# Queries of the attention heads formed transposed, copied out by ScalarE and rotated on VectorE behind the keys

## The chip, the core and the metric

The kernel runs on one core of one Trainium2 chip. Its engines run side by side and wait for each other by semaphores: TensorE (PE in the profile; PEld is its weight load), VectorE (DVE), ScalarE (ACT), GpSimd (POOL) and SyncE (SP), which issues most DMAs. The metric is the device time of one execution in microseconds (us), lower is better.

## The reference, cut to what matters

One inference step of a hybrid encoder layer: 512 prompt tokens and 32 sample tokens, model width 1024, 8 heads with two query and two key parts of 64 each (q1|q2, k1|k2) and values of 128, float32.

```
z = rms_norm(x) @ w_in            # pool branch 512 | q 1024 | k 1024 | v 1024 | gate logits 2048
q = rope_partial(q)               # first 16 of every 64 dims: x1*cos - x2*sin, x2*cos + x1*sin
k = rope_partial(k)               # k and v are outputs too (new_k, new_v); q is not
a = softmax(q1 k1) - lam * softmax(q2 k2)      # 64-token chunks, block-causal mask
attn = a @ v                      # then per-head RMSNorm
merged = sigmoid(g_A) * (pool_y @ w_pool_branch) + sigmoid(g_B) * (attn @ w_attn_branch)
x = x + merged @ w_out
x = x + hier_moe(rms_norm(x))     # 16 experts, 2 per token
```

## The kernel before, in words

Every float32 product is made of three: each operand is split into a high part (rounded to the `fp32r` type, by ScalarE) and a low part (the rest, by VectorE), and `three` (L1748 to L1750) adds high·high, high·low and low·high in PSUM. PSUM has eight banks of 512 float32 columns by 128 partitions (`ps`).

The order of work is written out by hand, one program for each engine, tied by counting semaphores. The stages are: the norm and the transposed activations `hTh`/`hTl` (channels on partitions, 544 tokens along the row); pool branch and first gates; the eight heads; the second gates; output projection; routing; the experts.

**Projection of a head** (`project(h, j)`, j = 0 to 7, 128 input channels each). For each of five token tiles (four of the prompt, tile 4 with the 32 sample tokens, through `dec`) the tokens are the stationary operand and the head's 384 columns q|k|v of the weights the moving one: 3 matmuls of 384 columns for tiles 0 to 3, 2 for tile 4, so 14 for each j and 112 for a head. Tile t accumulates in bank t; ScalarE copies each bank out (`evacuate`, L804) to `qkv`, tokens on partitions. VectorE adds the low half of the sample rows (`join_sample`, L1313) and rotates queries and keys together (`rope`, L1324 to L1329: six operations of 128x160).

**Attention of the head before it.** While PE projects head h, attention of head h-1 goes on in banks 5 to 7, between the tiles: `turn` transposes queries and keys (11 transposes, L1915 to L1922), ScalarE and VectorE split them (`attend`), `scores` (L1935) forms the logits of three groups of tiles, VectorE takes maxima, ScalarE exponentials (`exponentials`, L837), VectorE subtracts the second map (`probs`, L1284), `turn_probs` (L1944) transposes the probabilities, ScalarE and VectorE split them (`probs_hi` L826, `probs_lo` L1307), and `values` (L1953, L1954) multiplies by the values. The end of head h-1 reaches into the projection of head h+1: `values` of its second group stand behind tile 0 of j=0, `turn_probs` of the third group behind tile 4 of j=0, and `values` of the third behind tile 3 of j=1:

```
project(h, 0, {0: lambda: values(h - 2, 1), NT - 1: lambda: turn_probs(h - 2, 2)})
project(h, 1, {3: lambda: values(h - 2, 2)})
turn(h - 1)
```

Engines execute in program order, so on VectorE `probs_lo(h-2, 2)`, which `values(h-2, 2)` waits for, stands between `join_sample(h-1)` and `rope(h-1)`. PE may write tile t of head h only when its bank's copy is done (`acc_ev`), and tile 4 when `join_sample` is done as well (`dec_done`). Heads 2 to 6 run in a hardware loop; heads 0, 1 and 7 are written out. After the last projection come the blocks of the second gates (`gate_block`), of which the first writes banks 0 and 1.

## Time and profile before

| | us |
|---|---|
| median of 3 runs | 845.56 (845.19 to 846.67) |
| span of the profiled execution | 843.6 |
| one head in the loop, on PE | 28.52 (230.91 to 259.43 of the span) |
| PE busy | 821.1 (97%) |
| DVE busy | 588.7 (70%) |
| ACT busy | 512.7 (61%) |

The profile is of one execution. The times of the runs are some 2 us longer than its span, since they hold what lies around the first and last instruction. Matmuls are pipelined: the busy time of one (0.34 us for 384 columns) is about twice its distance to the next, and what a matmul costs a full PE is that distance.

### The profile page before, as it was taken

To read this page: it belongs to the slowest core of one execution; us is meant where nothing else is said; L and a number is where in the kernel's file an instruction comes from. 1 tells how busy PE (TensorE), PEld (TensorE's weight loads), DVE (VectorE), ACT (ScalarE), POOL (GpSimd) and SP (SyncE) were. 2 spreads that over 40 slices of the span, in tenths; PEclk is the share of its full clock that TensorE was granted. 3 is DMA by queue.
4 is the path that set the end of the run, shared out by engine and by line. 5 is a ranking of instruction groups with operands and counts; after the bars stand their busy time and mean duration, and the time that the engine had idled before them with its cause. 6 is when DMAs were issued, how large, how long until landed. Compare 5 with 4: busy or idle time off the path is not lost.

```text
span 843.6 us, 15839 instructions
## 1 busy us (share of the span) xinstructions
PE 821.1 (97%) x5378; PEld 748.1 (89%) x5378; DVE 588.7 (70%) x957; ACT 512.7 (61%) x935; POOL 87.6 (10%) x76
## 2 busy tenths in 40 slices
PE   8999999999999999999999999999999999999992
PEld 7999999999999999999999888888888888888881
DVE  6373332777677768467467126999989999989995
ACT  7343313666566656565525233488888887888884
POOL 0000000000000000000000001222223322223112
PEclk9999999999999999999999999999999999999996
DMA  9632213232133213332234746699999999999925
GB/s 274 139 103 83 67 44 95 82 109 75 36 104 107 59 54 108 102 101 75 79 123 157 270 177 204 236 371 372 380 377 374 368 368 367 364 368 367 351 70 193
DMA packets 135959, 163.54 MB, mean 194 GB/s; under 512 B 18599, under 2 KB 103719, under 8 KB 135914
## 3 DMA queue, kind: packets, MB, share of 16 engines
q1 hardware_dynamic: 129674, 149.53, 52.7%
q0 software_dynamic: 5952, 12.82, 5.4%
q8 instruction: 28, 0.46, 0.2%
q10 hardware_dynamic: 288, 0.59, 0.2%
q14 instruction: 17, 0.14, 0.1%
HBM read 151.61 MB, written 20.12 MB: 204 GB/s over the span
## 4 chain that ended last, share of the span: by engine, by line
PE 52%; DVE 3%; DMA 2%; issue 1%; ACT 1%; POOLq 0%; POOL 0%; ACTq 0%
PE ps L1748 15%; PE ps L1750 15%; PE ps L1749 15%; PE ps L2182 2%; PE ps L2094 1%; DMA xg<-sum_rows,idi 1%; PE ps L2101 1%; PE ps L2204 1%; DMA sum_rows<-yb,ydn 1%; PE ps L2086 0%; PE ps L2127 0%; PE ps L2128 0%; PE ps L2025 0%; DVE wl L1144 0%; PE ps L1953 0%
## 5 line engine op out<-in xcount | busy, mean ns | idle before, releaser
L1623 DVE TENSOR_TENSOR wl<-rawM,wh 128x1024 fp32r<-128x1024 f32 x189 | 223.9, 1220 | 14.3 <-ACT wh L980 12.4
L980 ACT ACTIVATE wh<-rawM 128x1024 fp32r<-128x1024 f32 x192 | 195.8, 1057 | 6.2 <-PE ps L1750 2.8
L1748 PE MATMUL ps<-hTh,wh 128*128 128x272 f32 (+2 forms) x448 | 131.0, 292 | 1.4 <-ACT qkv L804 1.0
L1750 PE MATMUL ps<-hTh,wl 128*128 128x272 f32 (+2 forms) x448 | 129.5, 289 | 0.0
L1749 PE MATMUL ps<-hTl,wh 128*128 128x272 f32 (+2 forms) x448 | 128.9, 288 | 0.0
L1748 PE MATMUL ps<-wh,xh 128*128 128x256 f32 (+1 forms) x384 | 124.3, 324 | 0.3 <-DVE xl L1669 0.3
L1750 PE MATMUL ps<-wh,xl 128*128 128x256 f32 (+1 forms) x384 | 121.7, 317 | 0.0
L1749 PE MATMUL ps<-wl,xh 128*128 128x256 f32 (+1 forms) x384 | 121.6, 317 | 0.0
L1748 PE MATMUL ps<-wh,hTh 128*128 128x384 f32 x256 | 90.0, 352 | 0.2 <-DVE mA L1254 0.2
L1748 PEld LDWEIGHTS ps<-hTh,wh 128*128 128x128 f32 x448 | 84.3, 188 | 3.0 <-ACT qkv L804 1.3
L1750 PE MATMUL ps<-wh,hTl 128*128 128x384 f32 x256 | 86.3, 337 | 0.0
L1749 PE MATMUL ps<-wl,hTh 128*128 128x384 f32 x256 | 86.0, 336 | 0.0
L1749 PEld LDWEIGHTS ps<-hTl,wh 128*128 128x128 f32 x448 | 84.4, 188 | 0.0
L1750 PEld LDWEIGHTS ps<-hTh,wl 128*128 128x128 f32 x448 | 84.3, 188 | 0.0
L1748 PEld LDWEIGHTS ps<-wh,xh 128*128 128x128 f32 x384 | 72.1, 188 | 9.9 <-issue 3.9
L1144 DVE TENSOR_TENSOR wl<-rawA,wh 128x1024 fp32r<-128x1024 f32 (+2 forms) x41 | 47.7, 1169 | 43.5 <-ACT wh L691 43.3
L1750 PEld LDWEIGHTS ps<-wh,xl 128*128 128x128 f32 x384 | 72.4, 188 | 5.8
L1749 PEld LDWEIGHTS ps<-wl,xh 128*128 128x128 f32 x384 | 72.3, 188 | 5.8
L691 ACT ACTIVATE wh<-rawA 128x1024 fp32r<-128x1024 f32 (+2 forms) x41 | 41.1, 1018 | 45.4 <-PE ps L1750 30.1
L605 POOL DMA_INDIRECT sum_rows<-yb,ydn x15 | 37.7, 2514 | 192.4 <-issue 167.0
L614 POOL DMA_DIRECT2D h_rows<-hb x4 | 2.4, 602 | 519.5 <-DVE hb L1484 519.5
L1748 PE MATMUL ps<-wh,hh 128*128 128x512 f32 x128 | 53.2, 415 | 0.6 <-DVE hl L1638 0.6
(324 smaller groups left out, 1711.5 us busy)
## 6 DMA issues: line engine op xcount, KB each, us to landing
rawM<-in_w_expert_up SPq DMA_DIRECT2D x64, 512.0 KB, 9.2
rawM<-in_w_expert_down SPq DMA_DIRECT2D x64, 512.0 KB, 8.0
rawM<-in_w_expert_gate SPq DMA_DIRECT2D x64, 512.0 KB
rawA<-in_w_in SPq DMA_DIRECT2D x64, 192.0 KB, 3.0
rawA<-in_w_in SPq DMA_DIRECT2D x20, 512.0 KB, 5.3
rawA<-in_w_attn_branch SPq DMA_DIRECT2D x8, 512.0 KB, 3.5
rawA<-in_w_out SPq DMA_DIRECT2D x8, 512.0 KB, 4.2
x<-in_x_prompt SPq DMA_DIRECT2D x4, 512.0 KB, 6.7
```

The source lines that it names most:

```text
L605: pool.indirect_dma_start(acc_rows[:, :], bass.IndirectOffsetOnAxis(ap=ydn[:, par:par + 1], axis=0), yb[:, par, :], None, bounds_check=TOK ...
L691: nc.scalar.activation(split_slot(n)[0][:, 0:w], rawA[:, n % RA, 0:w], ACT.Copy).then_inc(hi_done, 1)
L980: nc.scalar.activation(wh[:, (c + 1) % S, :], rawM[:, slot, :], ACT.Copy).then_inc(m_hi, 1)
L1144: V.tensor_tensor(l[:, 0:w], rawA[:, n % RA, 0:w], h[:, 0:w].bitcast(F32), ALU.subtract).then_inc(lo_done, 1)
L1623: V.tensor_tensor(wl[:, sl, :], rawM[:, slot, :], wh[:, sl, :].bitcast(F32), ALU.subtract).then_inc(m_lo, 1)
L1748: T.matmul(out, sh, mh_, start=start, stop=False, **kw)
L1749: T.matmul(out, sh, ml_, start=False, stop=False, **kw)
L1750: return T.matmul(out, sl, mh_, start=False, stop=stop, **kw)
L2094: ins = T.matmul(ps[:, 6 + m, 20 * i:20 * i + 20], h2T[:, 4 * (s % 2) + k, :], wr[:, 4 * m + k, :], start=k == 0, stop=k == 3)
L2101: T.matmul(ps[:, bank, :], one, many, start=True, stop=True)
L2182: ins = T.transpose(ps[:, 2 + k // 4, P * (k % 4):P * (k % 4 + 1)], xg[:, par, P * k:P * k + P], id_m)
L2204: ins = T.transpose(ps[:, 4, P * k:P * k + P], hid[:, P * k:P * k + P], id_m)
```

## The change: what it does

The queries leave the token-tile product. `queries(j, half)` takes the head's 128 query columns of the weights as stationary operand and 272 tokens of `hTh`/`hTl` as moving one, so queries come out transposed (dims on partitions, 544 tokens along the row) in banks 3 and 4. `keys_values(j, t)` does k|v, 256 columns, two token tiles to a bank (banks 0, 1, 2). `copy_queries` (ScalarE) copies both query banks to `q_turned`. The rotation of the queries is `swap_queries` and `turn_queries` on VectorE: two products of 128x544 with tables of cosines and signed sines, a `stream_shuffle` that swaps the two halves of 8 rows within each 32 partitions, and a sum. The tables (`q_cos`, `q_sin`, 544 columns each) are loaded once, ahead of the first cached keys. `rope` now rotates the keys alone (128x80), the transposes of the queries are gone from `turn`, and the splits of the values stand behind those of queries and keys. On VectorE `rope` and `swap_queries` now stand ahead of `probs_lo(h-2, 2)`. The copy of bank 0 waits for tiles 0 and 1. The hooks of `project` keep their numbers. Semaphores of the row loads are shared with the last stage's, which changes no order.

```diff
-        qkv = hr("qkv", [P, NT, 384])
+        kv = hr("kv", [P, NT, KV])
...
+        q_turned, q_swap, q_cos, q_sin = (at(n, 170 * K + 4 * TOK * b, [P, TOK]) for n, b in (
+            ("q_turned", 4), ("q_swap", 5), ("q_cos", 6), ("q_sin", 7)))
...
+        def kv_bank(t):
+
+            return ps[:, t // 2, KV * (t % 2):KV * (t % 2 + 1)]
...
+            sp.dma_start(q_cos[:], a["cst"][:, C_QCOS:C_QCOS + TOK]).then_inc(qt_in, 16)
+            sp.dma_start(q_sin[:], a["cst"][:, C_QSIN:C_QSIN + TOK]).then_inc(qt_in, 16)
...
-            def evacuate(h, tiles=range(NT)):
-
-                for t in tiles:
-                    if t < 4:
-                        act.wait_ge(acc_mm, 4 * h + t + 1)
+            def copy_queries(h):
+
+                act.wait_ge(q_mm, h + 1)
+                if not (isinstance(h, int) and h == 0):
+                    act.wait_ge(tr_lo, 2 * h)
+                nc.scalar.activation(q_turned[:].rearrange("p (h n) -> p h n", h=2), ps[:, 3:5, 0:HALF],
+                                     ACT.Copy).then_inc(q_ev, 1)
+
+            def evacuate(h, banks=range(NEV)):
+
+                for b in banks:
+                    if b < 2:
+                        act.wait_ge(acc_mm, 2 * h + b + 1)
                     else:
                         act.wait_ge(mm_done, H0 + 4 * h + 4)
-                    if t == 0 and not (isinstance(h, int) and h == 0):
+                    if b == 0 and not (isinstance(h, int) and h == 0):
                         act.wait_ge(kv_out, 64 * h)
                         act.wait_ge(tr_lo, 2 * h)
                         act.wait_ge(vlo_done, h)
-                    nc.scalar.activation(qkv[:, t, :], ps[:, t, 0:384], ACT.Copy).then_inc(acc_ev, 1)
+                    n = len(KV_TILES[b])
+                    nc.scalar.activation(kv[:, 2 * b:2 * b + n, :], ps[:, b, 0:KV * n].rearrange("p (t c) -> p t c", t=n),
+                                         ACT.Copy).then_inc(acc_ev, 1)
...
-                act.wait_ge(acc_ev, NT * (g + 1))
+                act.wait_ge(q_done, g + 1)
+                nc.scalar.activation(qh[:], q_turned[:], ACT.Copy).then_inc(q_hi, 1)
+                act.wait_ge(acc_ev, NEV * (g + 1))
                 if not (isinstance(g, int) and g == 0):
                     act.wait_ge(av_mm, NGR * g)
                 act.wait_ge(ckv_in, 32 * (g + 1))
                 act.wait_ge(dec_done, g + 1)
-                nc.scalar.activation(vh[:, 0:NT, :], qkv[:, :, 2 * P:3 * P], ACT.Copy)
-                nc.scalar.activation(vh[:, NT, :], ckv[:, 1, :], ACT.Copy).then_inc(vhi_done, 1)
                 act.wait_ge(tr_mm, 2 * g + 1)
-                nc.scalar.activation(qh[:, 0:SEQ], ps[:, 5, :], ACT.Copy)
                 nc.scalar.activation(kh[:], ps[:, 6, :], ACT.Copy).then_inc(tr_hi, 1)
                 act.wait_ge(tr_mm, 2 * g + 2)
-                nc.scalar.activation(qh[:, SEQ:TOK], ps[:, 7, LAST:P], ACT.Copy)
-                nc.scalar.activation(kth[:], ps[:, 7, P:3 * P], ACT.Copy).then_inc(tr_hi, 1)
+                nc.scalar.activation(kth[:], ps[:, 7, 0:2 * P], ACT.Copy).then_inc(tr_hi, 1)
+                nc.scalar.activation(vh[:, 0:NT, :], kv[:, :, P:KV], ACT.Copy)
+                nc.scalar.activation(vh[:, NT, :], ckv[:, 1, :], ACT.Copy).then_inc(vhi_done, 1)
...
+            def first_copies(h):
+
+                copy_queries(h)
+                evacuate(h, (0,))
...
             def join_sample(g):
 
-                dve.wait_ge(acc_ev, NT * (g + 1))
-                V.tensor_tensor(qkv[LAST:P, 4, :], ps[2 * DEC:LAST, 4, 0:384], qkv[LAST:P, 4, :],
+                dve.wait_ge(acc_ev, NEV * (g + 1))
+                V.tensor_tensor(kv[LAST:P, 4, :], ps[2 * DEC:LAST, 2, 0:KV], kv[LAST:P, 4, :],
...
+            def swap_queries(g, lk):
+
+                if isinstance(g, int) and g == 0:
+                    dve.wait_ge(qt_in, 32)
+                dve.wait_ge(q_ev, g + 1)
+                lk(V.tensor_tensor(q_swap[:], q_turned[:], q_sin[:], ALU.mult))
+                V.tensor_tensor(q_turned[:], q_turned[:], q_cos[:], ALU.mult)
+                lk(V.stream_shuffle(q_swap[:], q_swap[:], HALF_SWAP))
+
+            def turn_queries(g):
+
+                V.tensor_tensor(q_turned[:], q_turned[:], q_swap[:], ALU.add).then_inc(q_done, 1)
...
                 join_sample(h - 1)
+                rope(h - 1, lk)
+                swap_queries(h - 1, lk)
                 if not first:
                     probs_lo(h - 2, 2)
-                rope(h - 1, lk)
+                turn_queries(h - 1)
                 lo_head(2, n + 2)
...
+            def queries(j, half, sl, q0):
+
+                tc = slice(HALF * half, HALF * (half + 1))
+                return three(ps[:, 3 + half, 0:HALF], wh[:, sl, q0:q0 + P], wl[:, sl, q0:q0 + P], hTh[:, j, tc], hTl[:, j, tc],
+                             j == 0, j == KD - 1)
+
+            def keys_values(j, t, sl, q0):
+
+                wc, first = slice(q0 + P, q0 + 3 * P), j == 0 and t % 2 == 0
+                if t < 4:
+                    return three(kv_bank(t), hTh[:, j, col(t)], hTl[:, j, col(t)], wh[:, sl, wc], wl[:, sl, wc],
+                                 first, j == KD - 1, skip_group_check=True)
+                both = dec[:, 2 * DEC * j:2 * DEC * j + P]
+                T.matmul(kv_bank(t), both, wh[:, sl, wc], start=first, stop=False)
+                return T.matmul(kv_bank(t), both, wl[:, sl, wc], start=False, stop=j == KD - 1)
...
             def project(h, j, after={}):
 
                 n = H0 + 4 * h + j // 2
-                sl, k = (H0 + j // 2) % S, j % 2
-                if k == 0:
+                sl, q0 = (H0 + j // 2) % S, 384 * (j % 2)
+                if j % 2 == 0:
                     pe.wait_ge(lo_done, n + 1)
-                wc = slice(384 * k, 384 * k + 384)
+                if j == KD - 1:
+                    queries(j, 0, sl, q0)
+                    queries(j, 1, sl, q0).then_inc(q_mm, 1)
                 for t in range(NT):
-                    if j == 0:
-                        pe.wait_ge(acc_ev, NT * (h - 1) + t + 1)
+                    if j == 0 and t % 2 == 0:
+                        pe.wait_ge(acc_ev, NEV * (h - 1) + t // 2 + 1)
                         if t == 4:
                             pe.wait_ge(dec_done, h)
-                    if t < 4:
-                        ins = three(ps[:, t, 0:384], hTh[:, j, col(t)], hTl[:, j, col(t)], wh[:, sl, wc], wl[:, sl, wc],
-                                    j == 0, j == KD - 1)
-                    else:
-                        both = dec[:, 2 * DEC * j:2 * DEC * j + P]
-                        T.matmul(ps[:, t, 0:384], both, wh[:, sl, wc], start=j == 0, stop=False)
-                        ins = T.matmul(ps[:, t, 0:384], both, wl[:, sl, wc], start=False, stop=j == KD - 1)
-                    if j == KD - 1 and t < 4:
+                    ins = keys_values(j, t, sl, q0)
+                    if j == KD - 1 and t in (1, 3):
                         ins.then_inc(acc_mm, 1)
-                    if t == NT - 1 and k == 1:
+                    if j == KD - 1 and t == NT - 1:
                         ins.then_inc(mm_done, 1)
                     if t in after:
                         after[t]()
+                if j < KD - 1:
+                    if j == 0:
+                        pe.wait_ge(q_ev, h)
+                    queries(j, 0, sl, q0)
+                    ins = queries(j, 1, sl, q0)
+                    if j % 2:
+                        ins.then_inc(mm_done, 1)
 
...
-                for m in range(2):
-                    for t in range(4):
-                        ins = T.transpose(ps[:, 5 + m, P * t:P * t + P], qkv[:, t, P * m:P * m + P], id_m)
+                for t in range(4):
+                    ins = T.transpose(ps[:, 6, P * t:P * t + P], kv[:, t, 0:P], id_m)
                 ins.then_inc(tr_mm, 1)
                 if not (isinstance(g, int) and g == 0):
                     pe.wait_ge(av_ev, NGR * g)
-                for m in range(2):
-                    T.transpose(ps[:, 7, P * m:P * m + P], qkv[:, 4, P * m:P * m + P], id_m)
+                T.transpose(ps[:, 7, 0:P], kv[:, 4, 0:P], id_m)
                 pe.wait_ge(ckv_in, 32 * (g + 1))
-                T.transpose(ps[:, 7, 2 * P:3 * P], ckv[:, 0, :], id_m).then_inc(tr_mm, 1)
+                T.transpose(ps[:, 7, P:2 * P], ckv[:, 0, :], id_m).then_inc(tr_mm, 1)
...
-                if b < 2:
-                    pe.wait_ge(acc_ev, NT * (HEADS - 1) + 2 * b + 2)
+                if b == 0:
+                    pe.wait_ge(acc_ev, NEV * (HEADS - 1) + 2)
+                elif b == 1:
+                    pe.wait_ge(acc_ev, NEV * HEADS)
+                    pe.wait_ge(dec_done, HEADS)
+                    pe.wait_ge(q_ev, HEADS)
```

**VectorE, start of a head's body in the loop** (`project` of head h on PE; kv and rot are of head h-1, atl is the low part of the third group's probabilities of head h-2). Before:

```order
L1313 TENSOR_TENSOR qkv<-ps,qkv 32x384 [waits acc_ev]
L1307 TENSOR_TENSOR atl<-ps,ath 128x512 [waits ath_done]
L1324 TENSOR_TENSOR rot<-qkv,cst 128x160 [waits dec_done]
L1325 TENSOR_TENSOR rot<-qkv,cst 128x160
L1326 TENSOR_TENSOR rot<-qkv,cst 128x160
L1327 TENSOR_TENSOR rot<-qkv,cst 128x160
...
L1328 TENSOR_TENSOR qkv<-rot 128x5x4x8 [waits dve_chain]
L1329 TENSOR_TENSOR qkv<-rot 128x5x4x8
...
L1260 TENSOR_TENSOR wl<-rawA,wh 128x768 [waits hi_done]
```

and now:

```order
L1351 TENSOR_TENSOR kv<-ps,kv 32x256 [waits acc_ev]
L1375 TENSOR_TENSOR rot<-kv,cst 128x80 [waits dec_done]
L1376 TENSOR_TENSOR rot<-kv,cst 128x80
L1377 TENSOR_TENSOR rot<-kv,cst 128x80
L1378 TENSOR_TENSOR rot<-kv,cst 128x80
...
L1379 TENSOR_TENSOR kv<-rot 128x5x2x8 [waits dve_chain]
L1380 TENSOR_TENSOR kv<-rot 128x5x2x8
L1359 TENSOR_TENSOR q_swap<-q_turned,q_sin 128x544 [waits q_copied]
...
L1360 TENSOR_TENSOR q_turned<-q_turned,q_cos 128x544 [waits dve_chain]
L1361 STREAM_SHUFFLE q_swap<-q_swap 128x544
...
L1345 TENSOR_TENSOR atl<-ps,ath 128x512 [waits ath_done,dve_chain]
L1365 TENSOR_TENSOR q_turned<-q_turned,q_swap 128x544
```

The low part of the probabilities stood second, behind the sum of the sample rows; now six operations of the keys' rotation and three of the queries' stand ahead of it.

**ScalarE, end of the same body** (ps to qkv, kv and q_turned are copies out of the projection of head h; ath and E are of head h-1). Before:

```order
L801 REGISTER_ALU [waits acc_mm]
L802 REGISTER_ALU [waits kv_out]
L804 ACTIVATE qkv<-ps 128x384 [waits vlo_done,tr_lo]
...
L826 ACTIVATE ath<-ps 128x512 [waits ta_mm]
...
L837 ACTIVATE E_86,esum<-ps,nb 128x512 [waits nb_done]
...
L837 ACTIVATE E_86,esum<-ps,nb 128x512 [waits nb_done]
...
L804 ACTIVATE qkv<-ps 128x384 [waits acc_mm]
...
L804 ACTIVATE qkv<-ps 128x384 [waits acc_mm]
...
L804 ACTIVATE qkv<-ps 128x384 [waits acc_mm]
```

and now:

```order
L819 REGISTER_ALU [waits q_mm]
L820 ACTIVATE q_turned<-ps 128x544 [waits tr_lo]
...
L831 REGISTER_ALU [waits acc_mm]
L835 ACTIVATE kv<-ps 128x512 [waits vlo_done,tr_lo,kv_out]
...
L858 ACTIVATE ath<-ps 128x512 [waits ta_mm]
...
L869 ACTIVATE E_86,esum<-ps,nb 128x512 [waits nb_done]
...
L869 ACTIVATE E_86,esum<-ps,nb 128x512 [waits nb_done]
...
L835 ACTIVATE kv<-ps 128x512 [waits acc_mm]
...
L835 ACTIVATE kv<-ps 128x256 [waits mm_done]
```

Ahead of the split of the probabilities stood one copy of 384 columns, which waited for tile 0; now two copies of 544 and 512 columns stand there, and the second waits for tile 1. Behind the exponentials two copies are left of four.

**PE, the transposes between the second and third product of a head** (cst is the identity). Before:

```order
L1915 MATMUL ps<-cst,qkv 128x128 [waits exp_done]
L1915 MATMUL ps<-cst,qkv 128x128 x7
L1920 MATMUL ps<-cst,qkv 128x128 [waits av_ev]
L1920 MATMUL ps<-cst,qkv 128x128
...
L1922 MATMUL ps<-cst,ckv 128x128 [waits ckv_in]
```

and now:

```order
L1805 MATMUL ps<-hTh,wl 128x272
L1983 MATMUL ps<-cst,kv 128x128 [waits exp_done,rope_done]
L1983 MATMUL ps<-cst,kv 128x128 x3
L1987 MATMUL ps<-cst,kv 128x128 [waits av_ev]
...
L1989 MATMUL ps<-cst,ckv 128x128 [waits ckv_in]
```

Ten transposes of queries and keys have become five of keys alone; the cached keys' one stays, and a query matmul stands directly ahead.

## Rows read from the trace of the kernel before

**Rows 1.** The page's first part: busy time, share of the span, instructions of each engine.
```profile
PE 821.1 (97%) x5378; PEld 748.1 (89%) x5378; DVE 588.7 (70%) x957; ACT 512.7 (61%) x935; POOL 87.6 (10%) x76
```

**Rows 2.** The waits of PE over the span, third row: total, times, longest (us).
```profile
PE ps L1748 <- ACT qkv L804: 1.0, 1, 1.0
```

**Rows 3.** Windows: one period of the head loop; stretch, sum, busy by engine, clock, DMA.
```profile
230.91:259.43 28.52, 28.52 (x190) 26.59 (x189) 21.55 (x57) 18.31 (x59) 0.00 (x0) 1.00 0.28 79
```

**Rows 4.** Timeline, PE: start, us, engine, line; ten adjoining matmuls of 384 columns.
```profile
256.41 0.33 PE L1750 MATMUL ps<-wh,hTl 128*128 128x384 f32 x1
...
257.99 0.34 PE L1750 MATMUL ps<-wh,hTl 128*128 128x384 f32 x1
```

**Rows 5.** Timeline, PE: thirteen adjoining matmuls of 256 columns, weights as moving operand.
```profile
544.34 0.28 PE L1749 MATMUL ps<-wl,xh 128*128 128x256 f32 x1
...
545.70 0.28 PE L1749 MATMUL ps<-wl,xh 128*128 128x256 f32 x1
```

**Rows 6.** Timeline, PE: fourteen adjoining matmuls of 272 columns, gate logits.
```profile
340.27 0.29 PE L1749 MATMUL ps<-hTl,wh 128*128 128x272 f32 x1
...
341.90 0.29 PE L1750 MATMUL ps<-hTh,wl 128*128 128x272 f32 x1
```

**Rows 7.** Timeline, PE: twenty-four adjoining matmuls of 256 columns, activations as moving operand.
```profile
21.07 0.28 PE L1748 MATMUL ps<-hTh,wh 128*128 128x256 f32 x1
...
23.79 0.28 PE L1750 MATMUL ps<-hTh,wl 128*128 128x256 f32 x1
```

**Rows 8.** Timeline, PE: the transposes of one head's queries and keys.
```profile
259.43 1.04 PE L1915 MATMUL ps<-cst,qkv 128*128 128x128 f32 x8
260.31 0.38 PE L1920 MATMUL ps<-cst,qkv 128*128 128x128 f32 x2
```

**Rows 9.** Timeline, PE: from one head's last tiles to the next head's second product.
```profile
249.60 0.34 PE L1750 MATMUL ps<-wh,hTl 128*128 128x384 f32 x1
...
250.31 0.60 PE L1944 MATMUL ps<-cst,E 128*128 128x128 f32 x4
250.66 0.42 PE L1748 MATMUL ps<-wh,hTh 128*128 128x384 f32 x1
...
252.69 0.28 PE L1953 MATMUL ps<-vv,ath 128*128 128x256 f32 x1
...
253.57 0.39 PE L1748 MATMUL ps<-wh,hTh 128*128 128x384 f32 x1
...
258.16 0.28 PE L1953 MATMUL ps<-vv,ath 128*128 128x256 f32 x1
```

**Rows 10.** Timeline, ACT: the same stretch.
```profile
250.19 0.49 ACT L804 ACTIVATE qkv<-ps 128x384 f32<-128x384 f32 x1 [2.48 <-PE ps L1750]
250.94 0.60 ACT L826 ACTIVATE ath<-ps 128x512 fp32r<-128x512 f32 x1 [0.26 <-PE ps L1944]
251.44 0.68 ACT L837 ACTIVATE E<-ps,nb 128x512 f32<-128x512 f32 x1
...
252.76 1.64 ACT L804 ACTIVATE qkv<-ps 128x384 f32<-128x384 f32 x4
```

**Rows 11.** Timeline, DVE: the same stretch.
```profile
253.37 0.75 DVE L1284 SCALAR_TENSOR_TENSOR E<-E,ratio 128x512 f32<-128x512 f32 x1
254.44 0.56 DVE L1313 TENSOR_TENSOR qkv<-ps,qkv 32x384 f32<-32x384 f32 x1 [0.32 <-ACT qkv L804]
256.88 0.69 DVE L1307 TENSOR_TENSOR atl<-ps,ath 128x512 fp32r<-128x512 f32 x1 [1.88 <-ACT ath L826]
257.49 0.32 DVE L1324 TENSOR_TENSOR rot<-qkv,cst 128x160 f32<-128x160 f32 x1
...
259.02 0.95 DVE L1260 TENSOR_TENSOR wl<-rawA,wh 128x768 fp32r<-128x768 f32 x1
```

**Rows 12.** Groups of DVE instructions by line and form: count, busy us, mean ns.
```profile
L1334 DVE TENSOR_TENSOR vv<-qkv,vv 128x640 fp32r<-128x640 f32 x8 | 6.5, 819 | 3.4 <-ACT vv L850 3.4
...
L1335 DVE TENSOR_TENSOR vv<-ckv,vv 128x128 fp32r<-128x128 f32 x8 | 2.3, 287 | 0.0
```

109 lines of the change are left out of this document (60 added, 49 removed).

## The prediction

> **What bounds the kernel now.** I read the page's busy times first: PE is busy 97% of the span, VectorE 70%, ScalarE 61% [rows 1]. Then PE's waits: in the whole heads stage the only one listed is 1.0 us, once, where the first gate block needs the copies of banks 0 and 1 [rows 2]. A period of the head loop is 28.52 us with PE busy throughout, VectorE 21.55 and ScalarE 18.31, the clock granted in full [rows 3]. So today the stage is the sum of PE's own work, and the others have 7 and 10 us of air. But a mean says nothing about when. The timelines of the three engines side by side do: around the seam between two heads they form one long chain, from the last tiles of a head through the exponentials to `values` of the third group [rows 9 to 11]. That chain ends just in time today, and the change both lengthens it and shortens the PE work that covers it.
>
> **PE's own work, matmuls.** What one costs is the distance between starts. 384 columns: 1.58 us over 9 steps, 0.176 us [rows 4]. 256 columns with weights as the moving operand, which is the form of keys and values: 1.36 over 12 steps, 0.113 [rows 5]. 272 columns of activations, which is the form of the queries: 1.63 over 13, 0.125 [rows 6]. A 256-column form elsewhere takes 2.72 over 23, 0.118 [rows 7]. One input slice before is 14 x 0.176 = 2.46 us. After, it is 14 of 256 and 6 of 272: with 0.113, 1.59 + 0.75 = 2.34; with 0.118, 2.41. I take 0.115, since rows 5 have the operands of the new form: 2.36, a saving of 0.10 us. There are 8 slices in each of 8 heads: 6.2 us gained (3.2 to 7.7).
>
> A rule speaks against this step. The Trainium skill ("TensorE: Matmul & The Clock Gate", Back-to-back issue gap) gives a sustained 81 ns at 128 columns and 131 ns at 512 where each matmul loads weights, so much of the cost would not depend on width. My estimate from its straight line: 98 ns at 256, 100 at 272, 114 at 384, so a slice would go from 1.60 to 1.97 us and the 64 slices cost 24 us. The trace disagrees: 0.113 and 0.176 us stand nearly as 256 to 384 [rows 4, 5].
>
> **PE's own work, transposes.** `turn` loses five of its eleven. Eight took 0.88 us from start to the next kind, 0.11 each [rows 8]. 8 x 5 x 0.11 = 4.4 us gained. Matmuls and transposes together: 10.6 us, if PE never waits.
>
> **The chain at the seam.** Let T be the start of `turn_probs` of the second group, 250.31 [rows 9].
>
> ScalarE before: the copy of tile 0 starts 0.59 after the last matmul it waits for (249.60 to 250.19), is done early, and the split of the probabilities starts at T+0.63 [rows 9, 10]. After: the copy of bank 0 waits for tile 1, the last work ahead of T. A 256-column matmul is 0.06 shorter (0.28 against 0.34 [rows 5, 9]), so it starts 0.53 after a matmul that began at T-0.11: T+0.42. The copy of the queries stands ahead of it, but its product is 0.7 us older and it is over by then. A 512-column copy holds ScalarE 0.50 (250.94 to 251.44 [rows 10]). So the split starts at T+0.92 and the exponentials at T+1.42.
>
> VectorE: the map's subtraction ends 2.68 after the exponentials start (253.37 + 0.75 - 251.44 [rows 10, 11]): T+4.10. The next operation may start 0.08 before an unrelated one ends (256.88 + 0.69 against 257.49 [rows 11]). One more column costs 1.04 ns, (819 - 287)/512 [rows 12]. `join_sample`, 128 columns shorter than 0.56: T+4.02 to 4.45. The keys' rotation, six operations, took 1.53 (257.49 to 259.02 [rows 11]), and each loses 80 columns: 1.03, from T+4.48 to 5.51. A 544-column product is 0.287 + 416 x 1.04 ns = 0.72 [rows 12]. The first is waited for (0.04 more, from such pairs as the one above): T+6.27. The second, overlapping its follower by 0.08: T+6.91. The shuffle is not in the trace. Its nearest rows are those same sizes: 0.72 and the wait 0.04, T+7.67. Bounds: 0.29, the row of 128 columns, below [rows 12]; twice 0.72 above. Then the low split, 0.69 [rows 11]: T+8.36, and `values` can start at T+8.39.
>
> The Trainium skill ("VectorE: DVE Perf Modes", The perf-mode tier table) gives a shuffle of 2048 elements about 2400 ns where it gives the two-tensor product 2293, whatever the permutation. By that the shuffle is 0.1 us dearer than I take it, an estimate, and the time 0.6 us longer over six heads. No row here shows a shuffle.
>
> PE before: from T to `values` of the third group is 7.85 us (250.31 to 258.16 [rows 9]): 34 matmuls of 384 at 0.176 = 5.97, two `turn_probs` of 0.35, one `values` of 0.88 (252.69 to 253.57 [rows 9]), and 0.30 left over at changes of kind. The low split ended at 257.57, 0.6 ahead [rows 11]. PE after: 34 x 0.115 = 3.91, six query matmuls 0.75, and 0.70 + 0.88 + 0.30 as before: 6.54. So PE is there at T+6.54 and must wait until T+8.39: **1.85 us for each head.** Parts of it show earlier, and are in that sum, not beside it: `values` of the second group is wanted at about T+1.7, but its low split ends at 0.92 + 0.60 + 0.03 + 0.69 = T+2.24 [rows 10, 11], some 0.5 us; tile 4 is wanted near T+4.2 and the sample rows are joined at 4.45, some 0.3; the rest, about 1.0, at `values` of the third group.
>
> This hook runs in heads 2 to 7, six times: 11.1 us lost. Net for such a head: 0.8 + 0.55 gained, 1.85 lost, a period of 29.0 against 28.52.
>
> **Behind heads.** The first gate block waits for the second copy. Before that was over at T+2.94 (252.76 + 0.49, taken from the same seam), PE came at about T+1.9, hence the 1.0 us [rows 2, 10]. After, exponentials at T+1.42, the copy 1.32 later, 0.60 long: T+3.34, and PE comes at about T+1.4, since it has 0.5 us less to do: 1.0 us lost more.
>
> **Costed at nothing.** Behind the third `values`, VectorE has the queries' sum, a weight split, the two clamps and the low parts of queries and keys ahead of the first scores, some 4.0 us at these sizes; PE has `values`, tile 4, a query part, six transposes and a slice, 4.9. The value splits that moved back feed only the second half of the body. If that cover went it would cost the difference per head, up to 0.5. VectorE's total grows by some 2 us to 23.6 of 29.0, ScalarE's falls (one 544 copy and three, 1824 columns, for five, 1920). The two tables stand ahead of the first cached keys in SP's queue, under a DMA share of 0.28 [rows 3]: nothing, or some tenths once. Head 1 has no `values` and its seam should only close up.
>
> **Sum.** 843.6 - 6.2 - 4.4 + 11.1 + 1.0 = 845.1 for the profiled execution, 1.5 above its 843.6. The median lies 2.0 above that span, so 847.1.
>
> **Rivals.**
> - *Shorter chain.* If the rotation's operations on SBUF alone, small copies or waits are cheaper than read off and the chain from T to `values` is 7.6 instead of 8.4, each head waits 0.8 less: 842.3. For: I extrapolate four operations of 544 columns and six of 80. Against: the row of 640 columns is itself all in SBUF [rows 12]. The point from which the kernel is faster at all is a chain of T+8.1, so this is near. If VectorE were ready at T+6.54 nothing is lost in the loop, and 10.6 is gained: 835.0. That needs 1.85 us off the chain; the shuffle for nothing gives 0.76.
> - *The shuffle costs double.* 0.76 more for each of six heads, all of it on the chain: 851.7.
> - *A fixed part in each matmul.* If the new forms go at 0.118 [rows 7] the gain of the slices is 3.2 and not 6.2, but PE comes 0.1 later to each wait, 0.7 back: 849.4. Twenty matmuls for fourteen is what speaks for it. (The skill's rule above is the extreme of this; the trace leaves it no chance worth a number.)
> - *Waits pull the clock down.* Three waits of up to 1 us in each period; yet the present 1.0 us wait is followed at once by 272-column matmuls at 0.125 us, the full level [rows 2, 6]. No chance of its own.
>
> **Chances.** My forecast as worked out 0.55, from 844.3 to 850 for itself (0.3 of an us on the chain is 1.8 on the time); the shorter chain 0.17; no waits 0.05; double shuffle 0.11; fixed part 0.12. A measurement of this kernel tells about 0.2%, 1.7 us, from no change, so the line between same and slower is 847.25 and runs through my forecast. Slower: 0.27 of the forecast's share, 0.11 and 0.09: 0.47. Same: 0.22, 0.02, 0.03: 0.27. Faster: 0.06, 0.15, 0.05: 0.26. The range 842 to 851.5 leaves out the case without waits and the far halves of the short chain and of the double shuffle.
>
> **What would show it.** Starts of the 256-column matmuls 0.113 to 0.118 apart, of the query ones 0.125; five transposes of kv; PE waits named in the loop, where there were none: at `values` for atl, and at tile 4 for the joined rows, 1.85 us together; a loop period of 29.0; the shuffle near 0.72 us; the first gate block waiting about 2 us. The forecast is wrong if the loop period is at or below 28.5, if PE still shows no waits at the seam, or if the low split starts before T+7.4 because the operations ahead of it are shorter.

## The result, and the profile after

The changed kernel takes **851.1 us** (median of 4 runs, 850.92 to 851.65) against 846.1 of the kernel before on the same chip (845.19 to 846.77): ratio 1.0064, 95% interval 1.0052 to 1.0076, slower by 5.0 us. The forecast was 847.1, 1.5 slower. The side was right and the time lies in the range, 0.4 below its upper end, but the move is three times the one forecast. The profiled spans are 849.1 and 843.6, 5.5 apart.

The page's busy times after, for [rows 1]:

```profile
PE 817.7 (96%) x5722; PEld 746.3 (88%) x5722; DVE 606.2 (71%) x989; ACT 512.0 (60%) x919; POOL 87.5 (10%) x76
```

PE is busy 3.4 us less in a span 5.5 us longer. The waits of PE over the span (total, times, longest), for [rows 2]:

```profile
PE ps L2020 <- DVE atl L1345: 6.5, 12, 0.8
PE ps L1803 <- ACT kv L835: 1.6, 1, 1.6
```

A wait of the loop that was not there before heads the list: `values` (L2020) for the low split of the probabilities (`atl`), twice for each of six heads. The wait at the first gate block grew from 1.0 to 1.6. One period of the loop, `turn` to `turn`, for [rows 3] (stretch, length, busy by engine, clock, DMA):

```profile
233.55:263.09 29.54, 28.28 (x235) 26.48 (x234) 23.94 (x61) 18.33 (x57) 0.00 (x0) 1.00 0.27 77
```

A head takes 29.54 against 28.52, and 29.0 was forecast. The clock is granted in full in both. From `turn` to `turn` by the starts of PE's transposes, the first six periods sum to 176.98 us where they were 171.14: +5.84. The stretch ahead of the first `turn` is 0.23 shorter, the last period, with the first gate blocks, 0.21. So the loop holds the whole loss.

The seam between two heads on PE's timeline (idle time in brackets, and who ended it), for [rows 9]:

```profile
252.55 0.60 PE L2011 MATMUL ps<-cst,E 128*128 128x128 f32 x4
...
254.18 0.28 PE L1805 MATMUL ps<-wh,hTl 128*128 128x256 f32 x1
254.77 0.39 PE L2020 MATMUL ps<-vv,ath 128*128 128x256 f32 x1 [0.31 <-DVE atl L1345]
...
256.75 0.28 PE L1805 MATMUL ps<-wh,hTl 128*128 128x256 f32 x1
257.17 0.35 PE L1926 MATMUL ps<-wh,dec 128*128 128x256 f32 x1
...
259.99 0.28 PE L1805 MATMUL ps<-wh,hTl 128*128 128x256 f32 x1
261.07 0.38 PE L2020 MATMUL ps<-vv,ath 128*128 128x256 f32 x1 [0.80 <-DVE atl L1345]
```

Between starts, where 0.12 would pass without a wait, there are 0.59, 0.42 and 1.08 us: three delays of 0.47, 0.30 and 0.96 (the bracket names a part of the first and last, and none at tile 4), at the three places that the prediction named. And VectorE's in the same seam, for [rows 11]:

```profile
255.82 0.75 DVE L1322 SCALAR_TENSOR_TENSOR E<-E,ratio 128x512 f32<-128x512 f32 x1
256.60 0.42 DVE L1351 TENSOR_TENSOR kv<-ps,kv 32x256 f32<-32x256 f32 x1
257.06 0.24 DVE L1375 TENSOR_TENSOR rot<-kv,cst 128x80 f32<-128x80 f32 x1
...
258.10 0.72 DVE L1359 TENSOR_TENSOR q_swap<-q_turned,q_sin 128x544 f32<-128x544 f32 x1
258.86 0.73 DVE L1360 TENSOR_TENSOR q_turned<-q_turned,q_cos 128x544 f32<-128x544 f32 x1
259.51 0.01 DVE L1361 LOAD_MASK_SELECT q_swap<-q_swap  x1
259.51 0.78 DVE L1361 STREAM_SHUFFLE q_swap<-q_swap 128x544 f32<-128x544 f32 x1
260.32 0.69 DVE L1345 TENSOR_TENSOR atl<-ps,ath 128x512 fp32r<-128x512 f32 x1
```

There is no gap over 0.04 from the subtraction to the low split. With T = 252.55, the start of `turn_probs` of the second group as in the prediction, the split ends at T+8.46 and `values` starts at T+8.52; the forecast had T+8.36 and T+8.39. The chain was forecast to 0.13 us, so the size of the loss must come from the other side: from PE's own time.

### The profile page after: what moved, and what is told of

Its sections match the earlier page's. It is cut to its first block, busy times and chain, and to the rows that moved or that the text cites. A ratio compares the mean times of both kernels' runs of the same rounds, so it can differ in the third digit from the quotient of the medians.

```text
span 849.1 us, 16545 instructions
## 1 busy us (share of the span) xinstructions
PE 817.7 (96%) x5722; PEld 746.3 (88%) x5722; DVE 606.2 (71%) x989; ACT 512.0 (60%) x919; POOL 87.5 (10%) x76
## 4 chain that ended last, share of the span: by engine, by line
PE 52%; DVE 2%; DMA 2%; ACT 1%; issue 1%; POOLq 0%; POOL 0%; ACTq 0%
PE ps L1803 15%; PE ps L1805 15%; PE ps L1804 15%; PE ps L2252 2%; DMA xg<-sum_rows,idi 1%; PE ps L2164 1%; PE ps L2171 1%; PE ps L2274 1%; DMA sum_rows<-yb,ydn 1%; PE ps L2156 0%; PE ps L2197 0%; PE ps L2198 0%; PE ps L2095 0%; DVE wl L1182 0%; DMA out_y_prompt<-ob 0%
## 5 line engine op out<-in xcount | busy, mean ns | idle before, releaser
L1803 PE MATMUL ps<-hTh,wh 128*128 128x272 f32 (+2 forms) x576 | 168.2, 292 | 2.2 <-ACT kv L835 1.6
L1805 PE MATMUL ps<-hTh,wl 128*128 128x272 f32 (+2 forms) x576 | 166.4, 289 | 0.0
L1804 PE MATMUL ps<-hTl,wh 128*128 128x272 f32 (+2 forms) x576 | 165.9, 288 | 0.0
L1803 PEld LDWEIGHTS ps<-hTh,wh 128*128 128x128 f32 x576 | 108.5, 188 | 3.7 <-ACT kv L835 1.8
L1804 PEld LDWEIGHTS ps<-hTl,wh 128*128 128x128 f32 x576 | 108.6, 188 | 0.0
L1805 PEld LDWEIGHTS ps<-hTh,wl 128*128 128x128 f32 x576 | 108.4, 188 | 0.0
L1803 PE MATMUL ps<-wh,hTh 128*128 128x256 f32 x256 | 75.4, 294 | 0.1
L1805 PE MATMUL ps<-wh,hTl 128*128 128x256 f32 x256 | 72.1, 282 | 0.0
L1804 PE MATMUL ps<-wl,hTh 128*128 128x256 f32 x256 | 72.0, 281 | 0.0
```

Source lines behind the costliest of these rows:

```text
L1803: T.matmul(out, sh, mh_, start=start, stop=False, **kw)
L1804: T.matmul(out, sh, ml_, start=False, stop=False, **kw)
L1805: return T.matmul(out, sl, mh_, start=False, stop=stop, **kw)
```

## Experiments

All ratios are to the kernel before. Each was timed on one chip together with it, except the two kernels with a row of idle products, which ran once. Each changes the changed kernel, unless it says otherwise, and "theory A" and "B" are those of the expectation above each result.

### Is it the rotation that TensorE waits for?

First without it:

```diff
-                lk(V.tensor_tensor(q_swap[:], q_turned[:], q_sin[:], ALU.mult))
-                V.tensor_tensor(q_turned[:], q_turned[:], q_cos[:], ALU.mult)
-                lk(V.stream_shuffle(q_swap[:], q_swap[:], HALF_SWAP))
...
-                V.tensor_tensor(q_turned[:], q_turned[:], q_swap[:], ALU.add).then_inc(q_done, 1)
+                dve.sem_inc(q_done, 1)
```

> The changed kernel without the rotation of the queries: the two products, the shuffle and the sum on VectorE are left out (queries go into the scores unrotated), 3.0 us of VectorE work for each head ahead of the low split that the third value group waits for. Theory A (the rotation stands ahead of that split and TensorE waits for it 0.97 us in each turn of the loop, and starts again some 0.1 us late): the wait at the third value group goes, the waits at the second value group (0.3 to 0.5 us) and at tile 4 (0.4 us) stay, a head takes 28.45 us in place of 29.53, six of them 6.4 us less: 844.7 us. Theory B (the wait is set by the transposes and ScalarE's copies, not by the rotation): no change, 851. With either, what the head takes beyond its waits tells the pace of the products: 28.45 less 0.85 of waits is 27.6 with 256-column products at 0.119 us, and would be 27.2 at the 0.115 that the forecast took.

Measured: **844.65 us**, ratio 0.9983 (0.9973 to 0.9993). PE's waits, and a period:

```profile
PE ps L2017 <- DVE atl L1345: 1.7, 6, 0.3
...
PE ps L1800 <- ACT kv L835: 1.6, 1, 1.6
```

```profile
230.37:258.84 28.47, 28.00 (x235) 26.41 (x234) 21.27 (x55) 18.31 (x57) 0.00 (x0) 1.00 0.28 79
```

Twelve waits have become six, those of the second value group; the wait at the third is gone, and with it 1.06 us a head (28.47 for 29.53). Theory A stands to the tenth. But with the rotation left out and 0.8 us of wait left (0.5 at the second value group, 0.3 at tile 4), a head takes as long as before the change: 28.47 against 28.52. By the forecast's sizes it should have been 28.0: 28.52 less 0.77 for the slices and 0.55 for the transposes, and 0.8 of waits.

Then with more of it, the first product made twice:

```diff
                 lk(V.tensor_tensor(q_swap[:], q_turned[:], q_sin[:], ALU.mult))
+                lk(V.tensor_tensor(q_swap[:], q_turned[:], q_sin[:], ALU.mult))
```

> The changed kernel with the first of the rotation's products (queries by sines, 128x544, 0.72 us) made twice. Theory A (all of the rotation lies on the path to the third value group's low split): each of six heads gets 0.75 to 0.8 us longer, 4.5 to 4.8 us in all: 855.7 us, and TensorE's wait there grows from 0.97 to 1.75. Theory B (something beside VectorE sets that wait): below 852.

Measured: **859.16 us**, ratio 1.0151 (1.0136 to 1.0165): 8.1 over the changed kernel where 4.6 was expected. The direction is theory A's, the size is not. PE's waits, two of the periods, and then stretches of about one microsecond around another head's third value group, which starts at 266.62 (the clock is the third number from the end):

```profile
PE ps L2021 <- DVE atl L1345: 10.9, 12, 1.5
```

```profile
208.12:238.38 30.26, 28.27 (x235) 26.46 (x234) 24.60 (x62) 18.40 (x57) 0.00 (x0) 1.00 0.26 75
...
269.38:300.47 31.09, 29.12 (x234) 27.31 (x234) 23.92 (x61) 17.80 (x56) 0.00 (x0) 0.97 0.26 73
```

```profile
265.50:266.62 1.12, 0.00 (x0) 0.00 (x1) 1.08 (x3) 0.00 (x0) 0.00 (x0) 1.00 0.69 184
266.62:267.60 0.98, 0.98 (x9) 0.98 (x9) 0.98 (x2) 0.00 (x0) 0.00 (x0) 1.00 0.00 0
...
268.60:269.60 1.00, 1.00 (x7) 1.00 (x6) 0.96 (x2) 0.53 (x1) 0.00 (x0) 0.50 0.00 0
...
270.60:271.60 1.00, 1.00 (x9) 1.00 (x8) 0.50 (x1) 1.00 (x3) 0.00 (x0) 0.74 0.00 0
```

Two of the six periods are 0.73 longer than in the changed kernel, as worked out. The other four are 1.5 to 2.0 longer, and their mean clock is 0.97 or 0.98: behind two of the six waits of 1.5 us the granted clock falls from 1.00 to 0.50, the lower level of 1.2 GHz, for some 3.5 us (1.7 us lost), and each fall lies across a `turn`, so that it lengthens two periods. It was not this execution alone: the mean clocks of the five runs are 0.988 to 0.990, those of the changed kernel 0.992. The changed kernel's waits of 0.8 are followed by the full clock in every period, so this is no part of its loss. It is why a little more on that chain can cost double.

### The same work in other orders

One step moved: the low split ahead of the queries' rotation, behind the keys' (and likewise in the written-out last head).

```diff
                 rope(h - 1, lk)
-                swap_queries(h - 1, lk)
                 if not first:
                     probs_lo(h - 2, 2)
+                swap_queries(h - 1, lk)
                 turn_queries(h - 1)
```

> The changed kernel with one step moved: the third group's low split of the probabilities stands behind the rotation of the keys and ahead of the rotation of the queries. Theory A: the wait at the third value group goes (0.97 and 0.1 of restart), the queries' own splits come 0.7 us later and the first scores wait 0.3 us for them: a head takes 28.8 us in place of 29.53, in all 846.7 us (846 to 848). Theory B (the first scores wait for all that the value group no longer waits for, since the rotation is only shifted): the same as the changed kernel, 851. Were the products at the forecast's pace, this order would have come to 842.

Measured: **850.16 us**, ratio 1.0050 (1.0037 to 1.0064). A period, PE's waits, and VectorE's timeline behind the seam:

```profile
232.08:261.28 29.20, 28.13 (x235) 26.42 (x234) 23.64 (x61) 18.40 (x56) 0.00 (x0) 1.00 0.28 77
```

```profile
PE ps L2002 <- ACT E L869: 2.0, 6, 0.4
PE ps L2020 <- DVE atl L1345: 1.7, 6, 0.3
...
PE ps L2002 <- DVE kl L1387: 1.5, 6, 0.3
```

```profile
258.01 0.69 DVE L1345 TENSOR_TENSOR atl<-ps,ath 128x512 fp32r<-128x512 f32 x1 [0.57 <-ACT ath L858]
258.62 0.71 DVE L1359 TENSOR_TENSOR q_swap<-q_turned,q_sin 128x544 f32<-128x544 f32 x1
...
262.35 0.55 DVE L1309 TENSOR_TENSOR att<-att,clamped 128x384 f32 x1
...
268.85 0.16 DVE L1338 SCALAR_TENSOR_TENSOR nb<-mx,shift 128x2 f32<-128x2 f32 x1
...
270.15 0.18 DVE L1317 RECIPROCAL rinv<-esum 128x4 f32<-128x4 f32 x1 [0.35 <-ACT E L869]
```

The wait at the third value group went as expected, and 0.3 us at the first scores came as expected. What neither theory had is 0.4 us more at the second scores (L2002, which wait for the exponentials `E`): 2.4 us over six heads of the 3.5 by which 846.7 became 850.2; nearly 1.0 more came in the last period, 37.6 for 36.65. The reason is in the third fence: from 258.01 to 269.8 VectorE works without a gap over 0.04, so whatever is put in at the front arrives at the first maxima (`nb` at 268.85), and through the exponentials at the second scores. The loop has two chains, seam to values and seam to scores, and the rotation stands on both.

A second reordering moved the first clamp behind the splits, bank 0's copy behind the high split, and the first slice's queries and third transposes ahead of tile 4:

> The changed kernel with the same work in another order. VectorE: the third group's low split ahead of the queries' rotation, and the first clamp behind the splits of queries, keys and values. ScalarE: the copy of bank 0 behind the high split of the second group. TensorE: in the first slice of a head the queries' products and the third group's transposes stand ahead of tile 4. Theory A (what the change lost to its three waits of 1.8 us and two restarts of 0.1 us can all be had back, and what is left is TensorE's own work): a head takes 27.6 us (27.4 to 27.9), in all 839.5 us (838.5 to 841.5). With 256-column products at the forecast's 0.115 it would take 27.2 and come to 837. Theory B (the waits come back at another place, the first scores or the copies of the banks): 28.5 us or more, 845 us.

Measured: **853.8 us**, ratio 1.0089 (1.0073 to 1.0104). PE's waits from the first `turn` to the last:

```profile
PE ps L2001 <- ACT E L869: 7.0, 6, 1.2
PE ps L1800 <- ACT kv L835: 3.4, 7, 2.0
```

Theory B held: the value groups wait no longer (no `atl` in the list), and the time is lost at the second scores, 1.2 us a head, since the clamp still stood ahead of the maxima; a head takes 29.43. The 2.0 in the second row is the first gate block's. Behind it the granted clock was 0.50 for some 3.5 us in this profiled execution, which at 856.4 was the slowest of the four. Two versions that put the maxima first of all, and the clamp and a weight split behind them, were slower still (VectorE's lines that differ from the reordering before):

```diff
-                nxt(3)
                 largest(g, 0, lk)
                 if not (isinstance(g, int) and g == 0):
+                    clamp(g - 1, 0, lk)
                     clamp(g - 1, 1, lk)
+                nxt(3)
```

> The changed kernel with the third group's low split ahead of the queries' rotation, and with VectorE's line behind it shortened: the first maxima stand right behind the values' splits, and the clamp of three tiles and the next weights' low split behind them (2.0 us of work that no longer stands ahead of the maxima); ScalarE takes its first three squares behind the first exponentials. Theory A (in the version with the split moved alone, TensorE waited 0.3 us at the first scores and 0.4 at the second, because VectorE works from the third group's split to the first maxima, 12 us, without a gap; it is this line and no longer the third value group that sets the loop): both waits go, a head takes 28.4 us (28.3 to 28.6) with the waits at the second value group and tile 4 left, in all 844.7 us (844 to 846). Theory B (the line of VectorE is not what the scores wait for, ScalarE's exponentials and squares are): no gain over 850.2.

> The same as the version with the maxima first, and besides: ScalarE copies bank 0 behind the high split of the second group, and TensorE does the first slice's query products and the third group's transposes ahead of tile 4. Theory A (what is left then is TensorE's own work, 27.6 to 27.8 us a head): 840.2 us (839 to 842), below the kernel before. Were 256-column products at the 0.115 us of the forecast, it would be 837 to 838. Theory B (the copies of the banks or VectorE's line take over again): a head at 28.4 or more, 844.5 us or more.

Measured: **858.12** and **859.0 us**, ratios 1.0146 (1.0130 to 1.0162) and 1.0147 (1.0129 to 1.0164). PE's waits in the first of the two:

```profile
PE ps L2018 <- DVE atl L1345: 6.5, 12, 0.8
PE ps L1801 <- DVE wl L1182: 5.4, 2, 5.2
```

The scores wait no more, but the 2 us of work put behind the maxima now stands ahead of the first group's probabilities, and the first value group waits 0.8; and in the written-out tail the gate block's weight split is the work put behind, 5.2 us of wait at once. During that wait the granted clock fell to 0.50, and it stayed there until 372.8, 4.0 us after the wait's end: 2.0 us more. Both expectations missed because I looked only at who waits behind the front of the line, not behind its rear.

The third reordering was counted along the whole line. The clamp goes behind the first maxima, but the weight split stays ahead of them, where it fills the time until the scores are done; the next head's weight split goes behind the first low split; the second group's transposes go one tile earlier; the tail keeps its order. In the main:

```diff
                 largest(g, 0, lk)
                 if not (isinstance(g, int) and g == 0):
+                    if not last:
+                        clamp(g - 1, 0, lk)
                     clamp(g - 1, 1, lk)
...
                     probs_lo(g, i - 1)
+                    if not last and i == 1:
+                        nxt(4)
...
-                project(h, 7, {1: lambda: turn_probs(h - 1, 1)})
+                project(h, 7, {0: lambda: turn_probs(h - 1, 1)})
```

> The changed kernel's work in a third order. VectorE: the third group's low split ahead of the queries' rotation; the clamp of three tiles behind the first maxima (1.1 us less ahead of them), and the next head's first weight split behind the first group's low split (0.95 us less ahead of that). ScalarE: bank 0 copied behind the high split of the second group, the first three squares behind the first exponentials. TensorE: the second group's transposes one tile earlier (behind tile 0 of the last slice), the first slice's query products and the third group's transposes ahead of tile 4. The last head's own attention keeps its order. Theory A (counted along VectorE's line from the version of the first reordering: maxima end 17.4 us behind the second group's transposes, where TensorE wants the second scores at 17.4; first group's low split 22.0, wanted 22.5): no wait over 0.1 us is left in the loop, a head takes 27.7 us (27.5 to 28.0), in all 840.3 us (839 to 842.5), below the kernel before. Theory B (VectorE with 23.7 us of work in a head of 27.7 can't be kept off TensorE's path in any order): a head at 28.5 or more, 845 or more.

> The same as the shortened line, and for the last head ScalarE copies bank 1 with bank 0, ahead of the third group's exponentials, so that the first gate block, which TensorE waits 1.6 us for, finds its banks copied. Theory A: that wait goes to 0.2 us, the exponentials come 0.5 us later at a place with slack: 1.4 us below the version it is made from, 839. Theory B (the last head's attention is on the path that ends the stage, so that the 0.5 us come back): no difference.

Measured: **842.74 us**, ratio 0.9966 (0.9954 to 0.9979), and with bank 1 copied early for the last head **841.37 us**, ratio 0.9950 (0.9936 to 0.9963). Both are below the kernel before, by 0.3% and 0.5%, with intervals that leave out 1, and below the changed kernel. The early copy did what was expected of it: the wait of the gate block fell from 1.7 to 0.5 and the time by 1.4. The second one's waits of PE from the first `turn` to the last, whole list, and a period:

```profile
PE ps L1808 <- ACT kv L835: 0.5, 1, 0.5
PE ps L2009 <- ACT E L869: 0.2, 1, 0.2
```

```profile
229.02:257.07 28.05, 27.96 (x234) 26.46 (x233) 23.53 (x61) 18.33 (x56) 0.00 (x0) 1.00 0.28 81
```

So theory A is right in kind: VectorE with 23.5 of 28 us can be kept off PE's path. Its number was not: 28.05 us is some 0.35 more than expected, though PE has next to nothing left to wait for in the loop (all gaps are 0.2 or less). This is the cleanest reading of PE's own work in the new form, and it is only 0.47 below the old one.

### What a product costs

Does the price of 256 columns show in the time, and not only in the starts on the trace?

```diff
+                    if 2 <= j < KD - 1 and t < 4:
+                        keys_values(j, t, sl, q0)
                     ins = keys_values(j, t, sl, q0)
```

> The changed kernel with the 256-column products of the four prompt tiles made twice in slices 2 to 6 of heads 1 to 7 (the sums of keys and values are wrong by that): 12 x 5 x 7 = 420 products of 256 columns more on TensorE, and nothing on the other engines. Theory A (256 columns with weights moving cost 0.1187 us here, as the trace of the changed kernel shows): 49.9 us more, less up to 1 us where the waits of the gate block and of the loop find more slack: 900.5 us. With the forecast's 0.115: 48.3 more, 899.2; at the 0.1133 of the long runs in the last stage: 47.6 more, 898.5. The distance of two products in the trace, read in these runs of 24, is the sharper number: A says 0.119 or more.

Measured: **908.91 us**, ratio 1.0744 (1.0729 to 1.0758), 57.8 over the changed kernel. The expectation counted heads 1 to 7; head 0 runs the same function, so it is 480 products: 57.8/480 = 0.120 us each. The period of the loop gives the same without the rest:

```profile
262.42:299.15 36.73, 35.47 (x295) 33.67 (x294) 23.92 (x61) 18.40 (x57) 0.00 (x0) 1.00 0.22 62
```

36.73 - 29.53 = 7.20 for 60 products, 0.120. The forecast's 0.115 and the 0.113 of [rows 5] are out.

Why two prices for one shape? A row of idle products (their results are not used), one stationary operand, no waits:

> The changed kernel with a row of idle products put at its start, where no other engine has much to do, all of the same operands: 24 of 512 columns, 36 of 256, 8 transposes, 36 of 256, 24 of 272, 36 of 256, 24 of 384, 36 of 256, 12 of 288, 12 of 128, 36 of 256. The kernel gets some 40 us longer; only the distances of the products are read. Theory A (a 256-column product has two paces by what ran before it: 0.1133 us behind a run of 512 columns, 0.1178 to 0.119 behind transposes or 272 columns, and keeps it until another shape comes): 0.1133 in the first run of 36 and 0.118 in the others. Theory B (the pace hangs on how busy ScalarE, VectorE and the memory are): one pace in all five runs of 36. Theory C (it hangs on the stationary operand's layout, which is one and the same here): one pace as well.

Measured by stretches, from the first start of a run to the first of what follows (PE's count is one or two high, for products that reach in from the sides):

```profile
13.84:18.14 4.30, 4.30 (x37) 4.30 (x36) 0.00 (x0) 0.00 (x0) 0.00 (x0) 1.00 1.10 352
...
23.33:26.33 3.00, 3.00 (x26) 3.00 (x25) 0.00 (x0) 0.00 (x0) 0.00 (x0) 1.00 0.13 32
26.34:30.63 4.29, 4.29 (x38) 4.29 (x37) 0.00 (x0) 0.00 (x0) 0.00 (x0) 1.00 0.74 23
30.64:34.80 4.16, 4.16 (x26) 4.16 (x25) 0.00 (x0) 0.00 (x0) 0.00 (x0) 1.00 0.12 7
```

36 of 256 columns take 4.30 us, 0.1195, behind 512 and 272 columns alike (rows one and three), and the same behind 384. Behind transposes they take 4.38, but the 0.08 lie in the first step alone (0.20), and the last transpose has 0.03 to the next start where the others have 0.11. 24 of 272 take 3.00, 0.125; 24 of 384 take 4.16, 0.1735. Theory A is wrong. B and C foresaw the one pace, and neither explains the 0.113 of [rows 5], which stays open. The steps between widths are 128 columns in 0.054 us and 16 in 0.0055, so from 256 columns up a product costs its columns and, on top, a fixed 0.013 us: 256 columns at the 2.4 GHz level are 0.107, 384 are 0.160. Below 256 this does not hold: in the same row 12 products of 128 columns take 1.28 us, 0.107 each, where columns (0.053) and 0.013 would be 0.066.

Then whole slices, five old and five new, in the same way:

> The changed kernel with a row of idle products at its start, no waits among them and one bank, the stationary operand changed as in the heads: five old slices (14 products of 384 columns each), five new ones (14 of 256 and 6 of 272), then five times 4 transposes with 14 products of 256 behind them, and five times 4 transposes with 14 of 384. Only distances are read. Theory A (each product costs its columns and a fixed part of 0.013 us, as the idle row before showed: 0.1737 us for 384 columns, 0.1196 for 256, 0.1254 for 272): an old slice takes 2.43 us and a new one 2.43 as well, so that the products gain nothing where the forecast had 0.097 a slice; behind transposes both widths lose the same 0.1 us. Theory B (the fixed part belongs to products of one width alone, or to the heads' own conditions): a new slice at 2.36, 0.07 or more below an old one.

```profile
7.46:19.61 12.15, 12.15 (x71) 1.00 1.08 315
19.63:31.74 12.11, 12.11 (x101) 1.00 0.38 20
...
33.77:35.52 1.75, 1.75 (x17) 1.00 0.00 0
44.33:46.86 2.53, 2.53 (x17) 1.00 0.00 0
```

Five old slices take 12.16 us, 2.43 each; five new ones 12.12, 2.42 each. Behind transposes 14 of 256 take 1.76 and 14 of 384 take 2.54, both 0.1 over their pace. That is not a price of the change of kind: the last transpose is 0.08 short of its own. Four transposes with their 14 products take 2.11 and 2.90 us together (33.42 to 35.53, 43.97 to 46.87), and 4 x 0.109 and the products at their pace are 2.11 and 2.87. Theory A: **the new slice is worth nothing where nobody waits.** It has 160 columns less (14 x 384 - 14 x 256 - 6 x 272, 0.067 us) and six products more, 0.078 us of fixed parts.

The two kernels show the same where no attention stands among the slices, in the seven ahead of the first `turn`, before and after:

```profile
128.27:145.39 17.12, 17.12 (x99) 1.00 0.23 67
128.05:145.16 17.11, 17.11 (x142) 1.00 0.34 99
```

### One part alone

The kernel before with the values' splits moved behind the queries' and keys':

```diff
+                nc.scalar.activation(vh[:, 0:NT, :], qkv[:, :, 2 * P:3 * P], ACT.Copy)
+                nc.scalar.activation(vh[:, NT, :], ckv[:, 1, :], ACT.Copy).then_inc(vhi_done, 1)
                 nxt(3)
                 nxt(4)
```

(the same two lines taken out above, and on VectorE likewise)

> The kernel before with one part of the change alone: the splits of the values stand behind those of queries and keys on ScalarE and VectorE. Theory A (the forecast put nothing down for it: the kernel before has no wait of TensorE in the loop, and the queries' and keys' splits only come 1.1 us earlier): the same as the kernel before, within 0.2%. Theory B (the values' splits come later by the 2 us of the others, and the first value products or the next bank copy wait for them): slower by up to 1 us a head, 850.

Measured: 846.18 us, ratio 1.0008 (0.9999 to 1.0017), a head at 28.46. Theory A: no part of the loss comes from here, as forecast.

## Why the prediction was right or wrong

**Direction and mechanism: right.** PE, bound by its own work before, now waits at three places of the seam. Leaving the rotation out moves the wait and the time by what was worked out.

**The chain at the seam: right.** `values` at T+8.52 for T+8.39. The shuffle measured 0.78 us for 544 columns and the two products beside it 0.72. The Trainium skill ("VectorE: DVE Perf Modes", The perf-mode tier table) put a shuffle some 5% above such a product (about 2400 ns for 2293 at 2048 elements); here it is 8% above, 0.06 us. The prediction had made 0.1 us of it, since it took over the difference at 2048 elements as it stood; in proportion to 544 columns it is 0.03, an estimate from the same figures.

**Transposes: right.** From its first start to the next product's, `turn` went from 1.12 to 0.57 us, 4.4 us over eight heads.

**The slices: wrong, and this is the step that failed.** It read "With 0.113, 1.59 + 0.75 = 2.34; with 0.118, 2.41. I take 0.115", and booked 6.2 us (3.2 to 7.7). In the changed kernel two adjoining products of keys and values lie 0.119 apart, and 0.120 when more of them are timed. By distances in the trace a slice is then 14 x 0.119 + 6 x 0.125 = 2.41 against 2.46 of [rows 4], 2.8 us over 64 slices at most; the slices by themselves show 2.42 against 2.43, and seven slices ahead of the first `turn` 17.11 against 17.12: nothing. So of 6.2 us booked, between 0 and 2.8 were there. Taken whole, the starts of one period give 20.84 us to all products of a head before (changes of kind included), and 20.96 in the best version, of which up to 0.3 are waits of 0.2 or less. The upper half of the range, and the value in it, rested on [rows 5], a run of the last stage with other operands, where 0.118 of [rows 7] was the general price. The rival "a fixed part in each matmul" (849.4, chance 0.12) was the true case, and even its gain of 3.2 was more than any of these readings gives.

**The waits: right in size, but a term is missing.** Gaps between starts come to 0.47 + 0.30 + 0.96 = 1.73 us a head, for 1.85 forecast: the chain ended 0.13 later than forecast, and PE came 0.25 later (T+6.79, which is 8.52 less the gaps, for T+6.54). Over six heads that is 0.7 us less of wait, as the rival with the fixed part had it. But `values` behind a wait takes 0.98 us (254.77 to 255.75) where it took 0.88 (252.69 to 253.57 [rows 9]), twice a head: 0.2 us of restart each for six heads, 1.2 us, which the prediction had not at all and which more than ate the 0.7.

**First gate block:** 1.6 us of wait for 2.0 forecast, 0.4 better.

The account by these readings, against the profiled span: -2.8 (slices) -4.4 (transposes) +10.4 (waits) +1.2 (restarts) +0.6 (gate block) = +5.0, where the spans are 5.5 apart. The forecast had them 1.5 apart; of the 4.0 it missed by, the slices are 3.4, the restarts 1.2, and the waits and the gate block gave 0.7 and 0.4 back. Half a microsecond stays unplaced. The nearest place, not shown for all of it, is that the slices gain less than 2.8: those ahead of the first `turn` gained nothing.

**"Costed at nothing":** behind the third `values` I found VectorE's line to the first scores just covered, which held in the changed kernel, but only because the seam held PE back first. The first reordering took that away, and the line came up at the first and the second scores, 0.3 and 0.4 us. The prediction did not follow it so far.

## What to carry to other kernels

Price a matmul that is split into narrower ones with a fixed part for each (0.013 us here from 256 columns up, far more at 128), and take the pace from the stage and operands nearest to the new form, or the dearer of two rows, before booking a gain of a few per cent. When work is moved off the engine that bounds, follow the receiving engine's line of gapless work from end to end: here the rotation's 3 us on VectorE stood on two chains, and only an order that shortened both let the 4 us of saved transposes through. If a wait cannot be avoided, add the restart behind it (0.1 us here), and look at the granted clock behind it: here two of six waits of 1.5 us cost as much again in the clock.

## What was not expected of the hardware

- A 256-column product has one price, 0.1195 us, behind products of 512, 384 and 272 columns, with the other engines idle, and 0.119 to 0.120 in the heads; the 0.113 of the long runs in the last stage [rows 5] is the exception, unexplained.
- From 256 to 384 columns the cost rises by 0.054 us for 128 columns, the full rate, over the fixed 0.013; from 128 to 256 it rises by 0.0125 alone (0.107 to 0.1195). The Trainium skill ("TensorE: Matmul & The Clock Gate", Back-to-back issue gap) gives a sustained 131 ns at 512 columns. This case does not agree: in the first row of idle products 24 of them took 5.43 us, 0.226 each:

```profile
8.40:13.83 5.43, 5.43 (x25) 4.50 (x24) 2.55 (x4) 1.83 (x5) 0.00 (x0) 1.00 1.06 323
```

- Of six waits of 1.5 us at one place, two were followed by a granted clock of 0.50 for some 3.5 us, 1.7 us lost each time beside the wait; waits of 0.8 to 1.2 us in the same loop, in five kernels, by none. The wait at the first gate block was 1.6 to 1.7 us in seven kernels, none followed by a fall, and 2.0 us in two, both followed by one.
- A wait is dearer than its length: the eight products of a value group take 0.98 us right behind one and 0.88 otherwise. A change from transposes to products, which looks dear in the first product's step (0.20 for 0.12), costs nothing when the last transpose's (0.03 for 0.11) is counted with it.
